# Recurrent branch of a transformer block: norm sum and gate products later, recurrence in two parts around a convolution, GpSimd weight parts in four pieces

## The reference, cut to what matters

```python
h = rmsnorm_2(x, norm_mix_g[l])
u_x, u_g, q, k, v, g_lru, g_att = jnp.split(h @ w_in[l], split_idx, axis=-1)
c = causal_depthwise_conv(u_x, conv_w[l], conv_b[l])             # 4 taps along the tokens
r = sigmoid(blocks(c) @ w_r + b_r)                               # 16 blocks of 64 channels
i = sigmoid(blocks(c) @ w_i + b_i)
log_a = -8 * r * softplus(-lam)
a = exp(log_a)
u = sqrt(-expm1(2 * log_a)) * (i * c)
h_t = a_t * h_(t-1) + u_t                                        # along the tokens
y_lru = h * gelu(u_g)
```

## Time and profile before

| | before |
|---|---|
| median of 3 runs | 1878.95 us (1872.22 to 1880.02) |
| the profiled execution | 1881.36 us |
| its span in the trace | 1879.6 us |
| PE busy | 1742.2 us (93%), 8350 matmuls |
| DVE busy | 715.9 us (38%) |
| ACT busy | 607.1 us (32%) |
| POOL busy | 560.5 us (30%) |
| mean granted TensorE clock | 0.961 |

### The profile page before, as it was taken

One profiled execution on the slowest core, in us unless ns is written; L12 is line 12 of the kernel. 1 busy time (PEld: TensorE's weight loads), 2 busy tenths in 40 slices (PEclk: granted clock), 3 DMA queues, 4 the chain that ended last, 5 costly groups with the idle time before them and its releaser, 6 DMA issues.

```text
span 1879.6 us, 20344 instructions
## 1 busy us (share of the span) xinstructions
PE 1742.2 (93%) x8350; PEld 1217.4 (65%) x8350; DVE 715.9 (38%) x1053; ACT 607.1 (32%) x789; POOL 560.5 (30%) x239
## 2 busy tenths in 40 slices
PE   8778988599999999997879999999999999999995
PEld 5656666434444344435668896777778788888883
DVE  6555342523333433336961103323244421222335
ACT  4654333310010010115542136555333432322231
POOL 2312113222220122002234424443453344434430
PEclk9888889799999999999989999999999999999997
DMA  5211016289999999992122120202242232222201
GB/s 198 68 34 56 24 41 265 90 350 420 421 421 421 421 421 421 421 395 70 45 90 90 45 90 1 90 1 90 90 159 75 85 118 102 90 90 90 90 34 45
DMA packets 75068, 308.56 MB, mean 164 GB/s; under 512 B 3008, under 2 KB 4448, under 8 KB 50272
## 3 DMA queue, kind: packets, MB, share of 16 engines
q1 hardware_dynamic: 74704, 306.18, 41.7%
q0 software_dynamic: 272, 1.05, 0.2%
HBM read 305.12 MB, written 2.10 MB: 163 GB/s over the span
## 4 chain that ended last, share of the span: by engine, by line
PE 79%; DVE 11%; ACT 5%; issue 3%; POOL 2%; DMA 0%; DVEq 0%; SPq 0%; ACTq 0%
PE ps L837 38%; PE ps L1159 12%; PE ps L1183 6%; PE ps L879 6%; PE ps L1113 3%; PE ps L835 2%; PE ps L1306 2%; PE ps L1128 1%; PE ps L1129 1%; ACT sb_slot L1373 1%; PE ps L1291 1%; PE ps L1327 1%; ACT sb_R L1373 1%; DVE sb_R L2278 1%; POOL sb_w_parts L777 1%
## 5 line engine op out<-in xcount | busy, mean ns | idle before, releaser
L777 POOL TENSOR_TENSOR sb_w_parts<-sb_slot,sb_w_parts 128x2048 fp32r<-128x2048 f32 x59 | 274.3, 4650 | 412.7 <-ACT sb_w_parts L1373 412.7
L837 PE MATMUL ps<-sb_h_high,sb_w_parts 128*128 128x512 f32 x1120 | 275.4, 398 | 15.1 <-issue 8.2
L837 PEld LDWEIGHTS ps<-sb_h_high,sb_w_parts 128*128 128x128 f32 x1120 | 212.5, 191 | 67.2 <-issue 12.5
L1159 PE MATMUL ps<-sb_slot,sb_hT 128*64 128x512 f32 x768 | 171.1, 594 | 0.0
L1373 ACT ACTIVATE sb_w_parts<-sb_slot 128x2048 fp32r<-128x2048 f32 x59 | 112.6, 1911 | 172.4 <-PE ps L837 172.4
L837 PE MATMUL ps<-sb_hidden_high,sb_w_parts 128*128 128x512 f32 x704 | 165.2, 389 | 1.9 <-ACT sb_hidden_high L1373 1.9
L743 POOL TENSOR_TENSOR sb_tile_parts<-sb_slot,sb_tile_parts 128x1024 fp32r<-128x1024 f32 x32 | 77.9, 2437 | 250.2 <-ACT sb_tile_parts L1373 250.2
L837 PEld LDWEIGHTS ps<-sb_hidden_high,sb_w_parts 128*128 128x128 f32 x704 | 132.1, 188 | 29.7 <-ACT sb_hidden_high L1373 2.3
L837 PE MATMUL ps<-sb_h_low,sb_w_parts 128*128 128x512 f32 x560 | 138.2, 389 | 0.0
L1159 PEld LDWEIGHTS ps<-sb_slot,sb_hT 128*64 128x64 f32 x768 | 53.6, 137 | 106.2 <-issue 106.2
L837 PEld LDWEIGHTS ps<-sb_h_low,sb_w_parts 128*128 128x128 f32 x560 | 105.4, 188 | 22.0
(11 more groups left out here) (311 smaller groups left out, 2704.0 us busy)
## 6 DMA issues: line engine op xcount, KB each, us to landing
sb_slot<-w_up SPq DMA_DIRECT2D x24, 2048.0 KB, 15.8
sb_slot<-w_gate SPq DMA_DIRECT2D x24, 2048.0 KB, 15.7
sb_slot<-w_down SPq DMA_DIRECT2D x21, 2048.0 KB, 16.6
sb_slot<-w_in SPq DMA_DIRECT2D x14, 2048.0 KB, 8.0
sb_R<-w_down SPq DMA_DIRECT2D x11, 2048.0 KB, 16.0
sb_slot<-tiles SPq DMA_DIRECT2D x32, 512.0 KB, 3.5
sb_R<-w_gate SPq DMA_DIRECT2D x8, 2048.0 KB, 15.5
sb_R<-w_up SPq DMA_DIRECT2D x8, 2048.0 KB, 16.1
```

What stands on the lines that cost most here:

```text
L777: nc.gpsimd.tensor_tensor(low, raw_part(g), high.bitcast(F32), ALU.subtract).then_inc(w_low, 1)
L837: ins = nc.tensor.matmul(o, w[:, k, at:at + P], h[:, k, :], start=first, stop=last)
L1159: ins = nc.tensor.matmul(ps_[b * CAP:(b + 1) * CAP, bank0, :], xgT[:, k, at:at + CAP], w[:, b, kk * 512:(kk + 1) * 512], start=(k == 0), s ...
```

## The change

```diff
@@ -213,18 +213,18 @@
 
 
             if base in ("ux", "ug"):
-                pair = n // 2 - 1 + (4 if base == "ug" else 0)
-                if 0 <= pair < 4:
-                    if n % 2 == 0:
-                        for m in (2 * pair, 2 * pair + 1):
-                            job("lru_gate", "r", m)
-                            job("lru_gate", "i", m)
-                    elif base == "ug":
-                        step("lru", pair)
-                if base == "ux" and n % 2:
-                    step("conv", n // 2)
-                    if pair >= 0:
-                        step("lru", pair)
+                j = n + (KD if base == "ug" else 0)
+                if j < KD and j % 2 and j < 4:
+                    step("conv", j // 2)
+                if j % 2 == 0 and 4 <= j <= 10:
+                    for m in (j - 4, j - 3):
+                        job("lru_gate", "r", m)
+                        job("lru_gate", "i", m)
+                if j % 2 and 5 <= j <= 11:
+                    step("lru_in", (j - 5) // 2)
+                    if j < KD:
+                        step("conv", j // 2)
+                    step("lru", (j - 5) // 2)
             if base == "out2":
                 step("feed", 4, n)
             if base == "dn" and n >= 3 * KD:
@@ -422,6 +422,7 @@
         w_bd = view(R, 2048, KD, 2, P)
         sp8 = view(small, 16, KD)
         nsp8 = view(small, 24, KD)
+        nsp16 = view(small, 80, KD)
         lw = [view(small, 32 + 8 * i, KD) for i in range(6)]
         row_max, row_neg, row_sum, row_inv = (view(small, 96 + 4 * i, 2, 2) for i in range(4))
         dec = [view(small, 112 + 8 * i, 8) for i in range(2)]
@@ -774,7 +775,9 @@
 
                 high, low = weight_parts(g)
                 pool.wait_ge(w_high, g + 1)
-                nc.gpsimd.tensor_tensor(low, raw_part(g), high.bitcast(F32), ALU.subtract).then_inc(w_low, 1)
+                for k in range(0, KD, 2):
+                    ins = nc.gpsimd.tensor_tensor(low[:, k:k + 2, :], raw_part(g)[:, k:k + 2, :], high[:, k:k + 2, :].bitcast(F32), ALU.subtract)
+                ins.then_inc(w_low, 1)
 
             for st in steps:
                 if st[0] == "stick":
@@ -937,7 +940,7 @@
                     ins.then_inc(row_summed, 1)
                 elif kind == "proj":
                     project(*arg)
-                    if pending and arg in (("ux", 1), ("up", 1), ("pg", 1)):
+                    if pending and arg in (("ux", 2), ("up", 1), ("pg", 1)):
                         norm_sum(pending.pop())
                 elif kind == "lr":
                     o = begin(st)
@@ -1690,7 +1693,7 @@
                     finished(act, st)
                     dst, b_ = (lr_, "b_rgate_2") if which == "r" else (li, "b_igate_2")
                     frees(fn(dst[:, n % 2, :], bank(st), ACT.Sigmoid, bias=G(b_, n)), st)
-                elif kind == "lru":
+                elif kind == "lru_in":
                     g = arg[0]
                     if g == 0:
                         act.wait_ge(lam_done, 1)
@@ -1698,8 +1701,11 @@
                     taken(act, ("lru_gate", "r", 2 * g + 1))
                     for m in (2 * g, 2 * g + 1):
                         fn(la[:, m % 2, :], lr_[:, m % 2, :], ACT.Exp, scale=nsp8[:, m:m + 1])
-                        ins = fn(lt[:, m % 2, :], lr_[:, m % 2, :], ACT.Tanh, scale=sp8[:, m:m + 1])
+                        link(fn(lt[:, m % 2, :], lr_[:, m % 2, :], ACT.Tanh, scale=sp8[:, m:m + 1]))
+                        ins = fn(lr_[:, m % 2, :], lr_[:, m % 2, :], ACT.Exp, scale=nsp16[:, m:m + 1])
                     ins.then_inc(lru_exp, 1)
+                elif kind == "lru":
+                    g = arg[0]
                     act.wait_ge(lru_m2, g + 1)
                     fn(lt, lt, ACT.Sqrt).then_inc(lru_mult, 1)
                 elif kind == "stick":
@@ -1833,6 +1839,7 @@
                     link(v.tensor_scalar(lw[0], lam, -1.0, 0.0, ALU.mult, ALU.max))
                     link(v.tensor_tensor(lw[5], lw[5], lw[0], ALU.add))
                     v.tensor_scalar(nsp8, lw[5], -8.0, None, ALU.mult)
+                    v.tensor_scalar(nsp16, lw[5], -16.0, None, ALU.mult)
                     v.tensor_scalar(sp8, lw[5], 8.0, None, ALU.mult).then_inc(lam_done, 1)
                 elif kind == "lr":
                     finished(dve, st)
@@ -1913,6 +1920,8 @@
                         add_x(n, st)
                     elif name == "ux":
                         dve.wait_ge(pad_zero, 1)
+                        if n > 1:
+                            dve.wait_ge(conv_done, n - 1)
                         normed(uxp[:, n % 2, 3:3 + S], st)
                     elif name == "q2":
                         finished(dve, st)
@@ -2262,16 +2271,16 @@
                             if tap:
                                 link(ins)
                         ins.then_inc(conv_done, 1)
-                elif kind == "lru":
+                elif kind == "lru_in":
                     g = arg[0]
-                    dve.wait_ge(lru_exp, g + 1)
                     taken(dve, ("lru_gate", "i", 2 * g))
                     taken(dve, ("lru_gate", "i", 2 * g + 1))
                     dve.wait_ge(conv_done, 2 * g + 2)
-
-                    link(v.tensor_tensor(lr_, la, la, ALU.mult))
+                    link(v.tensor_tensor(li, li, lc[:, 2 * g % 4:2 * g % 4 + 2, :], ALU.mult))
+                    dve.wait_ge(lru_exp, g + 1)
                     v.scalar_tensor_tensor(out=lt, in0=lr_, scalar=1.0, in1=lt, op0=ALU.add, op1=ALU.mult).then_inc(lru_m2, 1)
-                    link(v.tensor_tensor(li, li, lc[:, 2 * g % 4:2 * g % 4 + 2, :], ALU.mult))
+                elif kind == "lru":
+                    g = arg[0]
                     dve.wait_ge(lru_mult, g + 1)
                     link(v.tensor_tensor(lt, lt, li, ALU.mult))
                     for m in (2 * g, 2 * g + 1):
```

## The result

The changed kernel takes 1886.68 us (median of 20 runs, 1881.25 to 1892.09), the kernel before, beside it, 1876.59 us (20 runs, 1871.94 to 1881.26). The ratio is 1.0053, with a 95% interval of 1.0040 to 1.0066: slower by 10.1 us. The profiled execution of the changed kernel has a span of 1887.3 us, against 1879.6.

The account below looks back on a forecast made before the run. The prediction took the recurrence, not PE, to bound the recurrent branch. It added 9 us there and 1 elsewhere to the median 1878.95, giving 1889 us, range 1871 to 1897 (main case 1884 to 1894).

Parts of the forecast that it names:

- Step 1: Start of the recurrent branch: norm sum behind ux 2 ends at 876.8, reciprocal at 881.1, first eviction 8.8 us later.
- Step 2: Convolution 0: five GpSimd pieces, 6.3 us, fall in it; ends about 894.5, unhindered 888.2; PE stands 4 us.
- Step 3: Pair 0 of the recurrence: item 4's four pieces add 5.0 us; done at 919.5, before the change at 907.1.
- Step 4: Recurrence turn of pair 1: 23.2 us against 18.5, convolution between lt and last product, item 5's pieces 5.0.
- Step 5: Turns of pairs 2 and 3: 19.5 us, before 22.6, one piece between scans; item 7's low part at 985.3.
- Step 6: PE at the branch's end: q2 starts 9 us later (8.7 unrounded); waits 5.5, 8, 6 before ug 2, 4, 6.
- Step 7: Weight parts outside the branch: hidden except at one PE wait of 2.51 us; +1 us, bounds 0 and 3.
- The third Exp: Recurrence turns: square of a leaves DVE (1.2 us less); ACT's six functions take 3.95 us, where four took 2.56.
- The port costs nothing: Rival: DVE's chained instructions win each border with GpSimd's pieces, 18.8 us off the recurrence, about 1870; chance 0.17.
- Half the price: Rival: a GpSimd piece costs a chained DVE instruction 0.55 us, not 1.25; 10 less, about 1879; chance 0.18.
- The slow clock lasts longer: Rival: PE's clock stays low a tile more behind the branch's last wait, 5.4 us on top, 1894; chance 0.15.

## Why the prediction was right, and where it was off

The forecast was +10 against the median, the measurement +10.1, with an interval of 7.5 to 12.4. Its mechanism holds: the late norm, the convolution in the chain of a turn, and GpSimd's pieces taking turns with DVE. That the two numbers agree to 0.1 us is luck, since errors cancel. In steps 2 to 4 the pieces are priced some 3.4 us too high, and against it stand a wait of DVE for TensorE (1.9) and slow passes that the sum doesn't have. By its steps (moments of the changed kernel are shifted by the 2.45 us that it came earlier to the copy of item 1):

- **Step 1, norm sum.** Ended at 876.8 as forecast, the reciprocal at 880.9 (881.1). The run that undid it gave 8.0 us back, for 8.8: 6.7 in the recurrence and 1.3 in TensorE's slow passes.
- **Step 2, convolution 0.** Ended at 893.2, forecast 894.5. Six pieces cost its instructions 5.3 us, 0.9 each, where I had five at 1.25. The rows that this price rests on the earlier trace rows didn't give it: the two instructions take 0.93 and 1.19 beside the pieces, and the other three of their size in this trace take 0.17, so 0.76 and 1.02 were added. I had put in the length of the piece. In the turns it is 0.9 a piece in the convolution and 1.07 for the last product. Piece and instruction follow one another every 1.6 to 1.7 us (6.50 / 4, 5.01 / 3), less than 1.25 + 0.75: some 0.35 of the two lie side by side. TensorE stood 2.70 in place of 4, halfway through the gate products.
- **Step 3.** Pair 0 done at 918.6, forecast 919.5. Near by cancelling: convolution 0 was 1.3 early and item 4's pieces cost 3.8 in place of 5.0, but DVE stood 1.88 for TensorE's tile ux 5, a wait that the step leaves out.
- **Step 4.** Turn of pair 1: 22.1, forecast 23.2, again the price of a piece.
- **Step 5.** Turn of pair 2: 19.6, forecast 19.5, with one piece between the scans. Item 7's low part at 983.9, forecast 985.3.
- **Step 6.** q2 8.1 us later in the branch, forecast 9 (8.7 before rounding). The step's own comparison gives 983.9 - 965.7 - 10.9 = 7.3 with the moment measured; the other 0.8 is the pass behind it, 2.95 in place of 2.17. Waits of 3.4 at ug 2 (5.5), 8.1 at ug 4 (8), 5.9 at ug 6 (6).
- **Step 7, elsewhere.** The wait in the MLP grew from 2.51 to 3.83, by 1.3 where I had worked out 1.1. It grew to 3.81 to 3.85 in all eight kernels with four pieces, and was 2.49 to 2.51 in all five with whole parts:

```profile
1478.42 3.65 PE L840 MATMUL ps<-sb_h_high,sb_w_parts 128*128 128x512 f32 x8 [3.83 <-POOL sb_w_parts L779]
```

What I had left out is the pass behind it, which ran at the slow clock, 3.65 in place of 2.12. From this moment to the end it is 408.9 to 409.0 us in all eight with four pieces; with whole parts it is 407.0 in two executions and 408.5 in three, in which this pass took 3.2 too. That is 2.0 of the 2.1 lost behind the branch, but the change makes it only by comparison with an execution whose pass was fast; against the other three it is 0.4. From q2 to this moment it is 479.4 us before and 479.5 after, so the 1.3 of the wait itself doesn't show there. Over all the executions this stretch scatters between 477.7 and 481.1 with whole parts and between 479.3 and 481.4 with pieces, and whether the 1.3 reaches the end stays open. So of the forecast's +1 elsewhere, no run shows that it is the change's.

- **The third Exp** (within steps 3 and 4): taken as even, and alone, in the old order, it is (0.2).

The rivals. *The port costs nothing* fell: leaving out three quarters of five parts was worth 14.7 us of the branch, and three chained instructions took 5.03 for 2.33. *Half the price* (0.55) lies below what was measured, 0.9 to 1.1, but in the convolutions the 0.9 is midway between it and my 1.25. *The slow clock lasts longer*: I had counted two slow passes at ug 4 and one each at ug 2 and ug 6, and they came (3.75 and 3.78, 2.96, 3.78). Beyond them the clock stayed low into the next pass for 0.8 us in the branch, not for a tile (5.4); of this kind, too, is the one pass in the MLP.

For a single waiting instruction the rows show that it waits for GpSimd's to end: two scans take 6.69 beside a whole part, 3.39 beside four pieces. The Trainium skill (SBUF — State Buffer, "Who interferes with whom") says that the engine that issues first holds the shared port for the whole instruction, and these rows agree. For a chain they show the engines taking turns at every border, so that all four pieces are paid, though not in full: a piece and an instruction together take 1.65 us, less than the 2.0 of the two lengths.

Where I was wrong was in the experiments that went on from there: twice I had the gain of earlier copies at 8 to 11 us, and it was 4.4 (two copies, whole parts) and 2.5 (one copy, on top of the four pieces), because another item's copy, behind the Gelus in ACT's queue, was late next.

## What to carry to other kernels

Before work is cut or moved off a slow instruction, look at what its neighbour on the port meets then: a GpSimd part cut in four saves three quarters of a lone wait and next to nothing in a chain of four or more DVE instructions. A price read from a row is the time added to the waiting instruction, not the length of the one that it waits for. A product that releases another engine's queue (here lt, then the root, then ACT's weight copy) is placed by what that queue triggers, not by when its inputs are ready. And where a copy stands in an in-order queue behind work of a chain, moving it ahead pays only down to the next copy that stands behind the same chain: list them all before working out the gain.

## What the hardware showed beyond that

- GpSimd loses at the port as well: four pieces take 5.0 us with no DVE chain beside them, 6.5 with convolution instructions between them, and 6.8 with scans, evictions and a product. Its whole part takes 4.6 alone and 5.0 to 5.1 beside a scan.
- A wait of TensorE costs more than its length. Behind waits of 2.5 us the next pass of eight took 2.1 in some executions and 3.2 in others of otherwise equal kernels; behind 3.8 us it took 3.3 to 3.8 in every one. At the wait of 2.5 in the MLP the clock granted over the 9 to 10 us around it was 1.00 in the execution of the kernel before and 0.81 to 0.83 in the three with a slow pass. Each slow pass adds 1.1 to 1.7 us, which a sum over waits doesn't hold.
- The moment at which ACT copies item 1 lay anywhere from 855.5 to 865.0 in the thirteen profiled executions, though no kernel changes more ahead of it than one small DVE instruction. A change of 0.3% is not seen in the span of one execution, but it is in the length of the stage.
